# A mixture-of-experts decoder step on one core: a fifth expert loaded ahead, the first four experts in straight code

## What is computed

```python
combine = jnp.sum(one_hot(flat_idx, 32) * ew[..., None], axis=1)
y = jnp.zeros_like(xf)
for e in range(32):
    he = silu(xf @ w_exp_gate[e]) * (xf @ w_exp_up[e])   # 1024 -> 256
    y = y + combine[:, e:e + 1] * (he @ w_exp_down[e])   # 256 -> 1024
```

## Time and profile before

| | |
|---|---|
| three runs, us | 633.28, 631.61, 633.42; median 633.28 |
| the profiled execution | 630.26 us; its span, from the first to the last instruction, 628.5 us |
| busy share of the span | PE 93%, PEld 82%, DVE 56%, ACT 30%, POOL 14% |
| mean granted TensorE clock | 0.968 of 2.4 GHz |
| DMA | 145.05 MB, 231 GB/s over the span |
| experts on PE (L1533 and L1547) | from 375.61 to 598.5 us |
| mixer and routing | up to 375.61 us; the end (turn, scatter, norm, stores) from 598.5 us |

### The profile page before, as it was taken

One profiled execution on the slowest core, in us unless ns is written; L12 is line 12 of the kernel. 1 busy time (PEld: TensorE's weight loads), 2 busy tenths in 40 slices (PEclk: granted clock), 3 DMA queues, 4 the chain that ended last, 5 costly groups with the idle time before them and its releaser, 6 DMA issues.

```text
span 628.5 us, 18681 instructions
## 1 busy us (share of the span) xinstructions
PE 583.0 (93%) x8085; PEld 518.3 (82%) x8085; DVE 348.9 (56%) x703; ACT 187.1 (30%) x312; POOL 85.3 (14%) x98
## 2 busy tenths in 40 slices
PE   4999999969979799999999879899999999999995
PEld 4577777747779798999777769899999999998973
DVE  2149997789989999977416983111111112121154
ACT  3121111463594162555317140012011121111152
POOL 2011000133539760014100000000000000000000
PEclk8599999989989899999999889999999999999999
DMA  9783425330333333360505907999999999999702
GB/s 251 248 248 144 163 70 199 135 133 1 135 135 135 135 135 135 135 202 3 201 0 195 408 1 264 413 399 424 421 422 422 422 421 423 422 422 421 317 2 75
DMA packets 41766, 145.05 MB, mean 231 GB/s; under 512 B 6966, under 2 KB 10278, under 8 KB 29430
## 3 DMA queue, kind: packets, MB, share of 16 engines
q1 hardware_dynamic: 33440, 140.88, 57.6%
q10 hardware_dynamic: 8294, 3.73, 2.5%
HBM read 143.02 MB, written 2.43 MB: 231 GB/s over the span
## 4 chain that ended last, share of the span: by engine, by line
PE 41%; DVE 11%; DMA 8%; issue 2%; ACT 1%; DVEq 0%; ACTq 0%
PE bank L1533 19%; PE bank L1547 8%; DMA ring<-w_exp_up 8%; PE bank L1421 5%; PE bank L1351 4%; PE bank L1581 2%; DVE w_lo L959 1%; PE bank L1447 1%; PE bank L1573 1%; DVE conv L1002 1%; DVE gel_lo L959 0%; DVE work L1033 0%; PE bank L1432 0%; DVE work L954 0%; DVE work L1014 0%
## 5 line engine op out<-in xcount | busy, mean ns | idle before, releaser
L1533 PE MATMUL bank<-work,ring 128*64 128x80 f32 x4096 | 150.8, 235 | 6.5 <-DMA ring<-w_exp_up 3.0
L1533 PEld LDWEIGHTS bank<-work,ring 128*64 128x64 f32 x4096 | 147.9, 140 | 7.6 <-issue 6.6
L1356 PE MATMUL bank<-work,ring 128*128 128x304 f32 x512 | 135.2, 425 | 0.9 <-ACT work L549 0.9
L1356 PEld LDWEIGHTS bank<-work,ring 128*128 128x128 f32 x512 | 98.8, 193 | 35.8 <-issue 2.9
L890 DVE SCALAR_TENSOR_TENSOR bank<-work,par,bank 128x272 f32<-128x272 f32 x232 | 96.4, 496 | 0.0
L1220 DVE TENSOR_TENSOR windows<-bank,outst 128x160 f32<-128x160 f32 x32 | 10.4, 325 | 133.6 <-ACT outst L769 133.6
L1547 PE MATMUL bank<-windows,ring 128*64 128x80 f32 x2048 | 77.3, 233 | 1.5 <-issue 1.5
L1547 PEld LDWEIGHTS bank<-windows,ring 128*64 128x64 f32 x2048 | 74.9, 137 | 1.6 <-issue 1.6
L959 DVE TENSOR_TENSOR w_lo<-ring,w_hi 128x2048 fp32r<-128x2048 f32 x17 | 40.2, 2367 | 15.7 <-ACT w_hi L630 15.7
L769 ACT ACTIVATE outst<-bank 128x160 f32<-128x160 f32 x32 | 9.7, 304 | 130.4 <-PE bank L1533 130.4
L1351 PE MATMUL bank<-xn_hi,w_hi 128*128 128x304 f32 x128 | 40.4, 315 | 7.0 <-DVE w_lo L959 3.7
(11 more groups left out here) (280 smaller groups left out, 797.4 us busy)
## 6 DMA issues: line engine op xcount, KB each, us to landing
ring<-w_exp_gate SPq DMA_DIRECT2D x32, 1024.0 KB, 13.8
ring<-w_exp_up SPq DMA_DIRECT2D x32, 1024.0 KB, 14.2
ring<-w_exp_down SPq DMA_DIRECT2D x32, 1024.0 KB, 15.3
ring<-w_in SPq DMA_DIRECT2D x11, 2048.0 KB, 8.5
ring<-w_rnn_proj SPq DMA_DIRECT2D x2, 2048.0 KB, 7.9
ring<-w_conv_proj SPq DMA_DIRECT2D x2, 2048.0 KB, 8.5
ring<-w_out SPq DMA_DIRECT2D x2, 2048.0 KB, 8.5
ring<-w_in SPq DMA_DIRECT2D x2, 1024.0 KB, 10.5
```

Of the source, the lines that this page charges most:

```text
L1356: ins = mm(bank[m % 4][:, 0:T], mix_w[b % MIX_SLOTS][:, i, (c % MB) * P:(c % MB + 1) * P], xnT[:, i], start=(i == 0), stop=(i == KT - 1))
L1533: ins = mm(bank[b][lo:lo + HP, (2 * m + f) * C:(2 * m + f + 1) * C], w_gu[s][m][:, k, f, lo:lo + HP], xw[b][:, k], start=(k == 0), stop=(k ...
```

## The change

- A fifth place for an expert's weights: gate in a new buffer `extra`, up and down at the front of `work` (`kept_up_down`). Expert 3 goes there and stays alone in it; its old place in `ring` takes expert 4. SP issues experts 0 and 2, waits for the logits (`log_mm`), issues 3 and 4, and then, still in straight code, the loads of 5, 6 and 7 as gate, up and down of experts 0, 1 and 2 are used. Only then does it wait for `over_done` and enter its loop, from expert 8 on.
- On PE, ACT and DVE the first four experts stand in straight code, ahead of the wait for `over_done`, the reading of `groups_i` and the loop, which now runs over the other experts (seven groups for 32 experts without overflow).
- On DVE the combine weights come first, then the first part of the overflow table (`overflow_places`, up to the places in `off_i`), then the first two slices. The second part (`overflow_experts`, which ends in `over_done`) comes after the slice that follows on expert 0.
- `gate_up` waits for the gate weights ahead of the gate half and for the up weights ahead of the up half.
- Buffers: `selT`, `logit` and the routing's intermediates are placed elsewhere, in `extra`, under `one_of` and in `outst`; the scratch for dynamic DMA is set to 2048 bytes.

The diff, cut to its core (unchanged bodies of moved steps left out):

```diff
-MAX_GROUPS = (NE + MAX_OVER + EXP_SLOTS - 1) // EXP_SLOTS
-ITEMS = MAX_GROUPS * EXP_SLOTS
+FIRST = 4
+KEPT, KEPT_SLOT = FIRST - 1, EXP_SLOTS
+GROUPS = (NE - FIRST) // EXP_SLOTS
+MAX_GROUPS = (NE - FIRST + MAX_OVER + EXP_SLOTS - 1) // EXP_SLOTS
+ITEMS = FIRST + MAX_GROUPS * EXP_SLOTS
+SCRATCH = 2048
...
+        extra = sb("extra", KT * F + PT * T)
...
-        at_xs = 0
-        xs_f = cut(KT * XS)
-        xs, xT2 = chan(xs_f), chan(xs_f[:, 0:KT * T])
+        kept_up_down = cut(KT * F + FT * D)
+        xT2 = chan(kept_up_down[:, 0:KT * T])
+        at_xs = KT * F + FT * D
+        xs = chan(cut(KT * XS))
...
-        cut(PT * T)
-        selT = rounded("selT", "work", at_sel + 2 * NT * SLOTS, PT * T)
-        logit = cut((NG + NE) * NT).rearrange("p (t e) -> p t e", t=NT)
-        el, oh1, oh2, rank, inw, rtmp = (cut(NE * NT).rearrange("p (t e) -> p t e", t=NT) for _ in range(6))
-        one_of = cut(MAX_OVER * NE * LEVELS).rearrange("p (i n) -> p i n", i=MAX_OVER)
-        item_at, item_no, item_on = (cut(NE * LEVELS).rearrange("p (e k) -> p e k", e=NE) for _ in range(3))
+        selT = rounded("selT", "extra", KT * F, PT * T)
+        router = cut(MAX_OVER * NE * LEVELS)
+        cut_r = cutter(router, 6 * NE * NT)
+        logit = extra[:, KT * F:KT * F + (NG + NE) * NT].rearrange("p (t e) -> p t e", t=NT)
+        el, oh1, oh2, rank, inw, rtmp = (cut_r(NE * NT).rearrange("p (t e) -> p t e", t=NT) for _ in range(6))
+        one_of = router.rearrange("p (i n) -> p i n", i=MAX_OVER)
+        item_on = cut(NE * LEVELS).rearrange("p (e k) -> p e k", e=NE)
...
+        w_gu_flat.append([extra[:, 0:KT * F], kept_up_down[:, 0:KT * F]])
+        w_dn_flat.append(kept_up_down[:, KT * F:])
...
+        item_at, item_no = (outst[:, at:at + NE * LEVELS].rearrange("p (e k) -> p e k", e=NE)
+                            for at in (9 * P - 2 * NE * LEVELS, 9 * P - NE * LEVELS))
...
-        gu_in = [sem(f"gu_in{s}") for s in range(EXP_SLOTS)]
-        dn_in = [sem(f"dn_in{s}") for s in range(EXP_SLOTS)]
+        gate_in, up_in, dn_in = ([sem(f"{n}_in{s}") for s in range(EXP_SLOTS + 1)] for n in ("gate", "up", "dn"))
...
+        def ring_slot(s):
+
+            return (s + FIRST - 1) % EXP_SLOTS
...
+                      .then_inc((gate_in, up_in)[m][s], 16)
...
-            for e in (0, 2, 3):
+            for e in (0, 2):
                 load_expert(e, e)
+            sp.wait_ge(log_mm, 1)
+            load_expert(KEPT, KEPT_SLOT)
+            load_expert(FIRST, EXP_SLOTS - 1)
+            load_gate_up(FIRST + 1, 0, 1)
+            load_gate_up(FIRST + 2, 1, 2)
+            load_down(FIRST + 1, 0, 1)
+            load_gate_up(FIRST + 3, 2, 3)
+            load_down(FIRST + 2, 1, 2)
+            load_down(FIRST + 3, 2, 3)
             sp.wait_ge(over_done, 1)
-            groups = sp.value_load(groups_i[0:1, 0:1], min_val=NE // EXP_SLOTS, max_val=MAX_GROUPS)
+            groups = sp.value_load(groups_i[0:1, 0:1], min_val=GROUPS, max_val=MAX_GROUPS)
             with sp.Fori(1, groups) as g:
                 for s in range(EXP_SLOTS):
-                    e = sp.value_load(exp_i[0:1, bass.ds(g * EXP_SLOTS + s, 1)], min_val=0, max_val=NE - 1)
-                    load_gate_up(e, s, g * EXP_SLOTS + (s + 1 - EXP_SLOTS))
+                    i = g * EXP_SLOTS + (s + FIRST)
+                    e = sp.value_load(exp_i[0:1, bass.ds(i, 1)], min_val=0, max_val=NE - 1)
+                    load_gate_up(e, ring_slot(s), g * EXP_SLOTS + (s + 1))
                     if s:
-                        load_down(last, s - 1, g * EXP_SLOTS + (s - EXP_SLOTS))
+                        load_down(last, ring_slot(s - 1), g * EXP_SLOTS + s)
                     last = e
-                load_down(last, EXP_SLOTS - 1, g * EXP_SLOTS)
+                load_down(last, ring_slot(EXP_SLOTS - 1), g * EXP_SLOTS + EXP_SLOTS)
...
+            for i in range(FIRST):
+                silu(i, i % 2)
+                if i:
+                    results(i - 1, (i - 1) % 2, results_at(i - 1))
+            results(FIRST - 1, 1, results_at(FIRST - 1))
             act.wait_ge(over_done, 1)
-            groups = act.value_load(groups_i[0:1, 0:1], min_val=NE // EXP_SLOTS, max_val=MAX_GROUPS)
+            groups = act.value_load(groups_i[0:1, 0:1], min_val=GROUPS, max_val=MAX_GROUPS)
...
+            def overflow_places():
...
+                    step.beside(vec.tensor_scalar(item_on[:, :, k], over, float(C * k), None, ALU.is_gt))
...
+                step(vec.tensor_copy(off_i[:, NE:NE + MAX_OVER], over_at))
+            def overflow_experts():
...
+                step(vec.tensor_copy(item_at, epri.unsqueeze(2).broadcast_to([P, NE, LEVELS])))
...
+                vec.tensor_copy(exp_i[:, NE:NE + MAX_OVER], over_e).then_inc(over_done, 1)
...
             for t in range(NT):
                 weights(t)
+            overflow_places()
...
+            for i in range(FIRST):
+                ahead = offset(i + 2)
+                hidden(i, i % 2)
+                window(ahead, i % 2)
+                if i == 0:
+                    overflow_experts()
+                else:
+                    results(i - 1, (i - 1) % 2, offset(i - 1))
+            results(FIRST - 1, 1, offset(FIRST - 1))
             dve.wait_ge(over_done, 1)
-            groups = dve.value_load(groups_i[0:1, 0:1], min_val=NE // EXP_SLOTS, max_val=MAX_GROUPS)
+            groups = dve.value_load(groups_i[0:1, 0:1], min_val=GROUPS, max_val=MAX_GROUPS)
...
 
                 pe.wait_ge(xw_done, windows)
-                pe.wait_ge(gu_in[s], loads)
                 for m in range(2):
+                    pe.wait_ge((gate_in, up_in)[m][s], loads)
                     for f in range(FT):
                         for k in range(KT):
...
+            for i in range(FIRST):
+                gate_up(i, i if i != KEPT else KEPT_SLOT, i % 2, 16, i + 1)
+                if i == 2:
+                    pe.wait_ge(wT_done, 4)
+                if i:
+                    down(i - 1, i - 1, (i - 1) % 2, 16)
+            down(KEPT, KEPT_SLOT, 1, 16)
             pe.wait_ge(over_done, 1)
-            groups = pe.value_load(groups_i[0:1, 0:1], min_val=NE // EXP_SLOTS, max_val=MAX_GROUPS)
+            groups = pe.value_load(groups_i[0:1, 0:1], min_val=GROUPS, max_val=MAX_GROUPS)
             with pe.Fori(0, groups) as g:
                 for s in range(EXP_SLOTS):
-                    gate_up(g * EXP_SLOTS + s, s, s % 2, g * 32 + 32, g * EXP_SLOTS + (s + 1))
-                    if s == 2:
-                        pe.wait_ge(wT_done, 4)
+                    i, loads = g * EXP_SLOTS + (s + FIRST), g * 16 + (32 if s else 16)
+                    gate_up(i, ring_slot(s), s % 2, loads, g * EXP_SLOTS + (s + FIRST + 1))
                     if s:
-                        down(g * EXP_SLOTS + (s - 1), s - 1, (s - 1) % 2, g * 16 + 16)
-                down(g * EXP_SLOTS + (EXP_SLOTS - 1), EXP_SLOTS - 1, 1, g * 16 + 16)
+                        down(g * EXP_SLOTS + (s + FIRST - 1), ring_slot(s - 1), (s - 1) % 2, before)
+                    before = loads
+                down(g * EXP_SLOTS + (EXP_SLOTS + FIRST - 1), ring_slot(EXP_SLOTS - 1), 1, before)
 
             keep_clock(0, 2)
-            pe.wait_ge(ys_act, groups * EXP_SLOTS + RESULTS_BEFORE)
-            pe.wait_ge(ys_dve, groups * EXP_SLOTS + RESULTS_BEFORE)
+            pe.wait_ge(ys_act, groups * EXP_SLOTS + (FIRST + RESULTS_BEFORE))
...
-    nc = bacc.Bacc("TRN2", target_bir_lowering=False, num_devices=1)
+    nc = bacc.Bacc("TRN2", target_bir_lowering=False, num_devices=1, dynamic_dma_scratch_size=SCRATCH)
```

More of the change, by code:

```diff
@@ L1175, in weights @@
                 dve.wait_ge(wsel_done, t + 1)
-            for k in range(LEVELS):
-                step.beside(vec.tensor_scalar(item_on[:, :, k], over, float(C * k), None, ALU.is_gt))
-                ins = vec.tensor_scalar(item_at[:, :, k], off[:, NE:], float(C * k), None, ALU.add)
-                step.beside(ins) if k < LEVELS - 1 else step(ins)
             flat = lambda ap: ap.rearrange("p e k -> p (e k)")
             each = lambda ap: flat(ap).unsqueeze(1).broadcast_to([P, MAX_OVER, NE * LEVELS])
-            step(vec.tensor_tensor_scan(flat(item_no), ones_b[:, 0:NE * LEVELS], flat(item_on), 0.0, ALU.mult, ALU.add))
@@ new lines, in overflow_experts @@
+            def overflow_experts():
+                step(vec.tensor_copy(item_at, epri.unsqueeze(2).broadcast_to([P, NE, LEVELS])))
+                step(vec.tensor_tensor(one_of, each(item_no), numbers, ALU.is_equal))
+                step(vec.tensor_tensor(one_of, one_of, each(item_at), ALU.mult))
+                step(vec.tensor_reduce(over_e, one_of, AX_X, ALU.add))
+                step(vec.tensor_scalar(over_e, over_e, -1.0, float(NE), ALU.mult, ALU.add))
+                step(vec.tensor_scalar(over_e, over_e, float(NE - 1), None, ALU.min))
+                vec.tensor_copy(exp_i[:, NE:NE + MAX_OVER], over_e).then_inc(over_done, 1)
```

54 lines of the change are left out of this document (26 added, 28 removed).

## The result

| | us |
|---|---|
| before, 20 runs | median 633.34 (630.07 to 638.45) |
| after, 20 runs | median 630.31 (627.30 to 637.46) |
| ratio after / before | 0.9943, 95% interval 0.9921 to 0.9964 |
| the profiled execution of after | 631.22; its span 629.5 |

The account below looks back on a forecast made before the run. PE's own work was taken to bound most of the expert stage, the load queue only its end. -3.45 - 2.4 + 4.0 + 0.5 - 4.2 = -5.55 us gave 624.7 profiled; with 3.0 carried over, 627.7 us, range 621.8 to 633.0.

Parts of the forecast that it names:

- Start, -3.45: PE's first expert matmul: with DVE's weights first and second table part moved back, PE starts at 372.2, 3.45 us earlier.
- Clock, -2.4: Start of the expert stage on PE: the half clock over the first 64 matmuls goes, saving 2.4 us.
- the hole up to 372.2 is 0.9 us instead of 4.3 in all: PE ahead of the first expert: back-to-back transposes at 369.0 to 371.3 leave 0.9 us idle, keeping the clock full.
- New code, +4.0: PE's instruction fetch: about 12 new code blocks instead of 6, the loop's first pass costing 4.0 us more.
- the lull that the prediction counted on: Load queue after experts 5 to 7: SP has nothing to issue until expert 4's gate has been used.
- fetch eats the gain: Rival on PE's new code: late at every block from the second on, +14.2, sum +4.65, 637.9 us; chance 0.12.
- fetch hidden: Rival on PE's new code: no block late, the queue bounds the end, -11.8, 621.5 us; chance 0.15.
- Reading the number of groups, +0.5: PE between straight code and loop: the reading, hidden at the start before, costs between 0 and 1.0 us.
- DMA waits at the end, -4.2: PE in the last experts: with five experts ready and 27 to load, the waits on up loads vanish, saving 4.2 us.
- 4.2 us of waits at most: Rival that the fifth expert does nothing: it removes at most these waits, never the 7.5 us off the queue; no chance given.
- Gate and up apart, 0: PE's separate waits for gate and up weights: worth nothing, and 2.2 us only if the queue were late.
- The margin of 2.3 us: Stage end: the last up load lands at 583.8, PE wants it at 586.1, so the queue is early by 2.3 us.

Follow-up runs that it names:

- experiment 1: The kernel before with only DVE's order changed (combine weights first, second table part later; SP still waits for the whole table): 632.28 us, ratio 0.9989 to before.
- experiment 2: The kernel of experiment 1 with gate and up released apart, no fifth place, no straight code: 629.99 us, ratio 0.9941 to before.
- experiment 3: After, with the loads of experts 5 to 31 and the waits for them left out: 619.48 us in one run.
- experiment 5: After without the fifth place, expert 3 back in its place in `ring`: 634.03 us, ratio 1.0011 to before.
- experiment 9: After with gate and up waited for together ahead of both halves: 631.52 us, ratio 0.9973 to before.
- experiment 6: After with 24 more instructions (idle matmuls) in PE's hole ahead of the first expert: 669.26 us, ratio 1.0541 to before.
- experiment 7: The kernel of experiment 2 with idle matmuls in PE's hole ahead of the first expert: 630.56 us, ratio 0.9963 to before.
- experiment 8: After with the idle matmuls of experiment 6, and the fill ahead of the gathers cut by as many instructions: 630.88 us, ratio 0.9967 to before.
- experiment 10: The kernel of experiment 2 with SP waiting for the table's second part only ahead of its last group of loads: 626.69 us, ratio 0.9899 to before.
- experiment 11: The kernel of experiment 10 with the first slices taken once the number of groups is known, the table's rest later: 624.29 us, ratio 0.9881 to before.
- experiment 4: The kernel before with only PE's first group of four experts written out ahead of its loop: 640.98 us, ratio 1.0105 to before.

## Why the prediction was right, and where it was not

The direction and the range held; of the forecast of -5.55 us the trace shows -2.17, and the medians 3.0. Step by step:

- **Start, -3.45: right.** -3.46 in the trace (the prediction's own rows add up to 3.40). The gathers and ACT's last move were hidden, as said, and experiment 1 has the same 14.0 us with nothing but DVE's order changed.
- **Clock, -2.4: the step failed in the profiled execution.** It rested on "the hole up to 372.2 is 0.9 us instead of 4.3 in all". The sum of DVE's times was right, but the transposes weren't: as one piece right behind the gathers (371.68 to 373.36) they took 1.68 us, where three rows of 0.76 had been added up, and so the hole behind them is 1.71 us long, while DVE does its last table steps and the value loads (1.87 in "issue" ahead of the slice). The granted clock was 0.60 over the first 4 us. By SP's first issue the gate half is 0.80 shorter, but the whole row of 256 matmuls only 0.43 (11.15 to 10.72): -0.43 for -2.4. At the full clock the row takes 9.08, so 2.07 were to be had. The same hole doesn't always cost this. Of six executions with the transposes in one piece and a hole of 1.7 to 1.8 us behind them, the first 256 matmuls took 10.72 us in four (after, experiments 2, 3 and 5) and 9.08 in two (experiments 1 and 9). So the term was mis-sized by 2.0 us in some executions and nearly right in others. In the five executions with a hole of 0.55 us or none (experiments 6, 7, 8, 10 and 11) the clock was full; in experiment 10 the hole was short only because the gathers ended 1.2 us later.
- **New code, +4.0: right in kind, too small.** Experiment 3 prices after's fetches at 9.2 us, against the 4.0 of before: +5.2. The straight code's three holes cost 4.3 us with the 0.23 each, where 4.0 were forecast; the loop's first pass, mid-stream, had three of about 1.4 us, 4.9 with the 0.23, again for 4.0. Without the lull that the prediction counted on, it would have been worse (experiment 5), and worse still with the kernel before's order of loads (experiment 4: 8.7 us more for six blocks more). The rival "fetch eats the gain" needed +9.6, so it didn't come; "fetch hidden" is refuted by after's own six late blocks and by the contrast of experiment 3.
- **Reading the number of groups, +0.5: right.** One hole of 0.20 us, 0.4 with the 0.23.
- **DMA waits at the end, -4.2: the number came out by luck, the reason was wrong.** All five are gone. But they are gone without a fifth expert too (experiment 5), and with it two come back when gate and up are waited for together (experiment 9). Straight code alone, without a fifth expert, also leaves two (experiment 4). So, as far as these runs go, a slower PE took away three of the five and the separate release the other two (after without both parts was not run). What the fifth expert is worth, 3.8 us in the trace of experiment 5 and 0.7% by the ratios, it gives by the queue's lull, through one late block fewer and, in that execution, a clock that doesn't fall. The prediction's remark that it removes "4.2 us of waits at most" had about the right size by another way.
- **Gate and up apart, 0: failed.** The margin of 2.3 us by which I saw the queue early already held the 2.2 us of the separate release ("less 2.2 for the gate"); without it nothing was left. Experiment 9 shows two waits come back, and by its trace and those of experiments 2 and 7 the separate release is worth 1.6 to 1.8 us, near the 2.2 that the prediction gave it for a queue that is late.
- **The sum.** -3.46 (start) - 0.43 (clock) + 5.2 (fetch) + 0.4 (reading) - 4.1 (waits) = -2.4, where the trace has -2.17. The 0.2 between them isn't placed. The two terms that were mis-sized, by 2.0 (clock) and 1.2 (fetch), are 3.2 of the 3.4 us by which the trace falls short of the forecast.

That after's median gained more (3.0 us, and 3.6 by the ratio) than its profiled execution from the mark on fits with a clock that is lost in some executions only, but no count over the 20 runs was made: that stays open.

## What to carry to other kernels

Code that an engine runs for the first time has a price when weights fill the DMA queues: here some 1.5 us for each block of 16 KB that came late (six of about twelve), and next to nothing when the queue was empty; so leave a first pass in the loop, or put new code where the queue rests. Before you count a gain from an earlier start, follow the engine that issues the loads to the wait that releases it: the same order on DVE, with gate and up apart, gave 0.6% with SP held back and 1.0% with SP freed. And when terms are summed, check that a margin does not already hold the gain of another part that you then price at nothing.

## What the runs showed of the hardware that was not expected

- 24 PE instructions ahead of a long loop cost 36 us (experiments 6 and 8), where the loop's end came to lie over the edge of a block: 45 instruction packets for 27, with holes of up to 6.9 us in the middle of a loop whose code had run before. With as many instructions taken away further up, the time was that of after again. Why the code is fetched again in bursts and not in each pass stays open.
- The same hole of 1.7 to 1.8 us ahead of the same matmuls was followed by the lower clock in four executions and by the full one in two.
- Holes in the middle of the stage went either way too. One of 2.05 us was followed by a granted clock of 0.57 over the next 4 us (experiment 5), and one of 1.91 us by 0.50 from 436.2 to 438.2 us (experiment 8), but those of 2.04 us (experiment 1), of 2.15 us (experiments 7 and 10) and of 1.78 us (after) by 1.00.
